# One ring of five for the raw and the lower halves of the weights, and the layer loop written out

## The reference

```python
for l in range(2):                                    # "the layers"
    a = hybrid_mixer(rms_norm(x), ...)                # MLA heads + dilated-window heads, w_in, w_uq, w_ukv, w_mix_out
    x = x + rms_norm(a)
    c = memory_cross_attention(rms_norm(x), mem, w_xq, w_xk, w_xv, w_xo)
    x = x + rms_norm(c)
    x = x + rms_norm(square(relu(rms_norm(x) @ w_up)) @ w_down)
...
# then one "second block": spatial gating + sparse attention with compressed keys,
# a memory attention and an MLP (w_ff1, w_ff2)
```

## Time and profile before

| | us |
|---|---|
| runs before | median 1491.85 of 3 (1487.62 to 1497.28) |
| span of the profiled execution | 1491.5 |
| device time of that same execution | not given apart; the median of the runs is 0.35 above the span |
| PE busy, DVE busy, ACT busy | 1339.5, 826.5, 665.9 |
| the layers and the second block, by their weights | to about 995, and from there |

### The profile page before, as it was taken

One profiled execution on the slowest core, in us unless ns is written; L12 is line 12 of the kernel. 1 busy time (PEld: TensorE's weight loads), 2 busy tenths in 40 slices (PEclk: granted clock), 3 DMA queues, 4 the chain that ended last, 5 costly groups with the idle time before them and its releaser, 6 DMA issues.

```text
span 1491.5 us, 24522 instructions
## 1 busy us (share of the span) xinstructions
PE 1339.5 (90%) x10217; PEld 1297.6 (87%) x10217; DVE 826.5 (55%) x872; ACT 665.9 (45%) x937; POOL 85.3 (6%) x65
## 2 busy tenths in 40 slices
PE   3998898889999899889888999989969888699999
PEld 3988897779999798889777999979969777699998
DVE  5476436456654547543645565456536765656542
ACT  5364334355543436433435454343234544355432
POOL 3000001020000100000202000003000000000000
PEclk7998999999999999889899999999659889899999
DMA  6633333235655533243333465565313123256553
GB/s 186 223 96 107 131 124 114 85 113 164 194 184 195 160 115 116 87 132 123 96 102 113 135 204 190 189 188 156 92 57 113 57 85 113 70 157 198 183 187 111
DMA packets 195585, 203.04 MB, mean 136 GB/s; under 512 B 5716, under 2 KB 191847, under 8 KB 195471
## 3 DMA queue, kind: packets, MB, share of 16 engines
q1 hardware_dynamic: 192704, 194.82, 40.8%
q0 software_dynamic: 2464, 5.99, 1.4%
q10 hardware_dynamic: 303, 0.61, 0.1%
HBM read 200.33 MB, written 3.16 MB: 136 GB/s over the span
## 4 chain that ended last, share of the span: by engine, by line
PE 75%; DVE 9%; ACT 8%; issue 6%; DMA 2%; POOL 0%; DVEq 0%; ACTq 0%; SPq 0%
PE bank L554 13%; PE bank L555 13%; PE bank L556 13%; PE bank L2033 6%; PE bank L2035 6%; PE bank L2031 6%; ACT w_hi L508 3%; PE bank L595 3%; DVE w_lo L518 3%; PE bank L596 2%; PE bank L597 2%; PE bank L1893 1%; PE bank L1954 1%; PE bank L1918 1%; DVE rstd L1251 1%
## 5 line engine op out<-in xcount | busy, mean ns | idle before, releaser
L518 DVE TENSOR_TENSOR w_lo<-raw,w_hi 128x2048 fp32r<-128x2048 f32 (+7 forms) x210 | 424.1, 2029 | 462.1 <-ACT w_hi L508 462.0
L508 ACT ACTIVATE w_hi<-raw 128x2048 fp32r<-128x2048 f32 (+7 forms) x210 | 354.7, 1703 | 481.1 <-PE bank L556 200.8
L554 PE MATMUL bank<-act_hi,w_hi 128*128 128x256 f32 x1096 | 313.2, 286 | 1.1 <-DVE act_lo L1718 1.1
L555 PE MATMUL bank<-act_lo,w_hi 128*128 128x256 f32 x1096 | 310.8, 284 | 0.0
L556 PE MATMUL bank<-act_hi,w_lo 128*128 128x256 f32 x1096 | 310.7, 283 | 0.0
L554 PEld LDWEIGHTS bank<-act_hi,w_hi 128*128 128x128 f32 x1096 | 211.0, 193 | 2.1 <-DVE act_lo L1718 1.9
L2031 PE MATMUL bank<-h_hi,w_hi 128*128 128x256 f32 x768 | 212.2, 276 | 0.0
L2033 PE MATMUL bank<-h_lo,w_hi 128*128 128x256 f32 x768 | 212.0, 276 | 0.0
L2035 PE MATMUL bank<-h_hi,w_lo 128*128 128x256 f32 x768 | 212.0, 276 | 0.0
L555 PEld LDWEIGHTS bank<-act_lo,w_hi 128*128 128x128 f32 x1096 | 211.1, 193 | 0.2
L556 PEld LDWEIGHTS bank<-act_hi,w_lo 128*128 128x128 f32 x1096 | 211.0, 193 | 0.0
(11 more groups left out here) (329 smaller groups left out, 2279.6 us busy)
## 6 DMA issues: line engine op xcount, KB each, us to landing
raw<-in_w_up_dram SPq DMA_DIRECT2D x32, 1024.0 KB, 5.4
raw<-in_w_down_dram SPq DMA_DIRECT2D x32, 1024.0 KB, 5.1
raw<-in_w_ff_dram SPq DMA_DIRECT2D x32, 1024.0 KB, 5.3
raw<-in_w_in_dram SPq DMA_DIRECT2D x23, 1024.0 KB, 5.3
raw<-in_w_xk_dram SPq DMA_DIRECT2D x8, 1024.0 KB, 5.1
raw<-in_w_xv_dram SPq DMA_DIRECT2D x8, 1024.0 KB, 5.1
raw<-in_w_mix_out_dram SPq DMA_DIRECT2D x8, 1024.0 KB, 5.2
raw<-in_w_xq_dram SPq DMA_DIRECT2D x8, 1024.0 KB, 5.1
```

The costliest lines, as they stand in the source:

```text
L508: ins = act.activation(d, r, ACT.Copy)
L518: ins = dve.tensor_tensor(d, r, h.bitcast(F32), ALU.subtract)
L554: pe.matmul(o, stat_hi, mov_hi, start=first, stop=False)
L555: pe.matmul(o, stat_hi, mov_lo, start=False, stop=False)
```

## The change

`raw` and `w_lo` become two names of the same memory, a ring of five slabs; `w_hi` stays a ring of three. DVE writes the lower half over the raw slab that it reads. Where the split rearranges columns (the seven kinds above) it can't be written in place: such a slab takes two places, one for raw and the next one for its lower half. A function counts this out beforehand for all 187 slabs. A place comes free when PE has used what lay in it, so SP's queue now waits on `slab_used` in place of `slab_lo`. With five places and no rearranged slab about, the load of slab s waits for used s-5; behind a rearranged one it waits for less distant ones. The table of the distances that result, from the function:

| slabs | the load waits for |
|---|---|
| layer, 0 to 2, and 16 to 63 | used s-5 |
| layer, 3 to 7, 14, 15 | used s-4 |
| layer, 8 and 9 | used 3 and 5 |
| layer, 10 | used 7 |
| layer, 11 and 12 | used 9, both |
| layer, 13 and 14 | used 10, both |
| second block, 4, 5, 6 | used 1, 2, 3 |
| second block, 7 | used 3 |

In layer 0 the first four loads wait for nothing. The loops over the layers are Python loops now, and all engines have straight code with constants in their waits. The order of the steps is the same on every engine.

```diff
-RAW = 2
-RING = 3
+HI_RING = 3
+LO_RING = 5
...
+def weight_places():
+
+    places, at, count, user = [], 0, [0] * LO_RING, [0] * LO_RING
+    for g in range(DEPTH * 64 + 59):
+        layer, s = min(g // 64, DEPTH), g - 64 * min(g // 64, DEPTH)
+        moved = s in ((3, 4, 9) if layer == DEPTH else (3, 9, 10, 11))
+        r, lo = at % LO_RING, (at + moved) % LO_RING
+        at += 1 + moved
+        count[r] += 2 if layer == DEPTH and s in (3, 4) else 1
+        places.append((r, lo, count[r], max(user[r], user[lo])))
+        user[r] = user[lo] = g + 1
+    return places
...
-        raw = sb("raw", [P, RAW, SLAB])
-        w_hi = sb("w_hi", [P, RING, SLAB], F32R)
-        w_lo = sb("w_lo", [P, RING, SLAB], F32R)
+        loads = ExitStack()
+        with loads:
+            raw = sb("raw", [P, LO_RING, SLAB], on=loads)
+        w_lo = sb("w_lo", [P, LO_RING, SLAB], F32R)
+        w_hi = sb("w_hi", [P, HI_RING, SLAB], F32R)
...
-            loads = s // RAW + 1 + (second(layer) and s >= 3)
-            act.wait_ge(raw_loaded[s % RAW], layer * (16 * 32) + 16 * loads)
-            if s >= 3:
-                last = s - 2 if second(layer) else {16: 16, 17: 14, 18: 15}.get(s, s - 2)
-                act.wait_ge(sig["slab_used"], value("slab_used", layer, last))
+            r, _, loads, _ = PLACES[64 * layer + s]
+            act.wait_ge(raw_loaded[r], 16 * loads)
+            if 64 * layer + s >= HI_RING:
+                act.wait_ge(sig["slab_used"], value("slab_used", layer, s - HI_RING + 1))
...
-                sp.wait_ge(sig["slab_lo"], value("slab_lo", layer, s - RAW + 1))
+                r, _, _, users = PLACES[64 * layer + s]
+                if users:
+                    sp.wait_ge(sig["slab_used"], users)
...
-            with sp.Fori(0, DEPTH) as layer:
+            for layer in range(DEPTH):
...
-            with act.Fori(0, DEPTH) as layer:
+            for layer in range(DEPTH):
```

More of the change, by code:

```diff
@@ L367, in build @@
         sig = {name: sem(name) for name in PER}
-        raw_loaded = [sem(f"raw_loaded{r}") for r in range(RAW)]
+        raw_loaded = [sem(f"raw_loaded{r}") for r in range(LO_RING)]
         i_load = {n: sem("i_" + n) for n in ("cst", "x", "mem", "gains", "pos", "relb", "rows", "skew", "toep", "gains_2",
@@ L488, in split_views, with of_hi, of_lo, of_raw @@
             return [(d[:, :, x0:x1], r[:, :, y0:y1]) for (x0, x1), (y0, y1) in pieces]
[L490 to L495, removed]
-        def split_hi(act, layer, s):
-            loads = s // RAW + 1 + (second(layer) and s >= 3)
-            act.wait_ge(raw_loaded[s % RAW], layer * (16 * 32) + 16 * loads)
-            if s >= 3:
-                last = s - 2 if second(layer) else {16: 16, 17: 14, 18: 15}.get(s, s - 2)
-                act.wait_ge(sig["slab_used"], value("slab_used", layer, last))
+        PLACES = weight_places()
+        def of_hi(layer, s):
+            return w_hi[:, (64 * layer + s) % HI_RING]
+        def of_lo(layer, s):
+            return w_lo[:, PLACES[64 * layer + s][1]]
+        def of_raw(layer, s):
+            return raw[:, PLACES[64 * layer + s][0]]
+        def split_hi(act, layer, s):
+            r, _, loads, _ = PLACES[64 * layer + s]
+            act.wait_ge(raw_loaded[r], 16 * loads)
+            if 64 * layer + s >= HI_RING:
+                act.wait_ge(sig["slab_used"], value("slab_used", layer, s - HI_RING + 1))
             pieces = split_views_2 if second(layer) else split_views
-            views = pieces(s if s < 64 else 0, w_hi[:, slot(layer, s)], raw[:, s % RAW])
+            views = pieces(s if s < 64 else 0, of_hi(layer, s), of_raw(layer, s))
             for n, (d, r) in enumerate(views):
@@ L515, in split_lo @@
             pieces = split_views_2 if second(layer) else split_views
-            for (d, r), (h, _) in zip(pieces(sp, w_lo[:, slot(layer, s)], raw[:, s % RAW]),
-                                      pieces(sp, w_hi[:, slot(layer, s)], raw[:, s % RAW])):
+            for (d, r), (h, _) in zip(pieces(sp, of_lo(layer, s), of_raw(layer, s)),
+                                      pieces(sp, of_hi(layer, s), of_raw(layer, s))):
                 ins = dve.tensor_tensor(d, r, h.bitcast(F32), ALU.subtract)
@@ L558, in w_view @@
         def w_view(layer, s, cols):
-            return (w_hi[:, slot(layer, s)].rearrange("p (k n) -> p k n", n=cols),
-                    w_lo[:, slot(layer, s)].rearrange("p (k n) -> p k n", n=cols))
+            return (of_hi(layer, s).rearrange("p (k n) -> p k n", n=cols),
+                    of_lo(layer, s).rearrange("p (k n) -> p k n", n=cols))
         def columns_slab(pe, layer, s, o, src_hi, src_lo, ready=None, first=True, last=True):
@@ L1367, in _ @@
             dve.wait_ge(i_evac, 8)
-            with dve.Fori(0, DEPTH) as layer:
+            for layer in range(DEPTH):
                 dve.tensor_copy(g_cur[:, :], g_all[:, layer, :]).then_inc(sig["gains"], 1)
@@ L1984, in slab @@
                     pe.wait_ge(sig["c_lo"], value("c_lo", layer, 5))
-                    wh = w_hi[:, slot(layer, s)].rearrange("p (a k n) -> p a k n", a=2, k=2)
-                    wl = w_lo[:, slot(layer, s)].rearrange("p (a k n) -> p a k n", a=2, k=2)
+                    wh = of_hi(layer, s).rearrange("p (a k n) -> p a k n", a=2, k=2)
+                    wl = of_lo(layer, s).rearrange("p (a k n) -> p a k n", a=2, k=2)
                     for m in range(4):
@@ L2039, in wh3 @@
             def wh3(layer, s):
-                return w_hi[:, slot(layer, s), 0:1536].rearrange("p (k n) -> p k n", k=3)
+                return of_hi(layer, s)[:, 0:1536].rearrange("p (k n) -> p k n", k=3)
             def wl3(layer, s):
-                return w_lo[:, slot(layer, s), 0:1536].rearrange("p (k n) -> p k n", k=3)
+                return of_lo(layer, s)[:, 0:1536].rearrange("p (k n) -> p k n", k=3)
             def kpe(layer, _):
@@ L2054, in _ @@
             steps = {"slab": slab, "pair": pair, "stat": stat, "kpe": kpe, "scores": scores, "turn": turn, "pv": pv, "ot": turn_o}
-            with pe.Fori(0, DEPTH) as layer:
+            for layer in range(DEPTH):
                 for kind, n in TE_ORDER:
@@ L2229, in slab_2 @@
                     pe.wait_ge(once["ch_lo"], 2)
-                    wh = w_hi[:, slot(DEPTH, s), 0:512].rearrange("p (k n) -> p k n", n=P)
-                    wl = w_lo[:, slot(DEPTH, s), 0:512].rearrange("p (k n) -> p k n", n=P)
+                    wh = of_hi(DEPTH, s)[:, 0:512].rearrange("p (k n) -> p k n", n=P)
+                    wl = of_lo(DEPTH, s)[:, 0:512].rearrange("p (k n) -> p k n", n=P)
                     for kind in range(2):
```

18 lines of the change are left out of this document (9 added, 9 removed).

## The result

The changed kernel takes 1514.16 us (median of 4 runs, 1510.34 to 1516.72) against 1493.11 for the kernel before in the same comparison (4 runs, 1487.62 to 1497.28). The ratio is 1.0152, with a 95% interval of 1.0127 to 1.0177: slower by 1.5%, 21 us. The forecast was 1503.0: the sign was right, the loss in the layers was foreseen and most of that in the second block was not, and the size was half of what came. The forecast gave 0.31 of chance to a loss of over 1%, and 0.64 to a result within 1%.

What follows compares the result with a forecast made beforehand. PE was taken to bound the kernel, busy 1339.5 of 1491.5 us. Terms 4.0 + 5.1 + 2.1 + 1.1 - 1.0 - 0.2 = 11.1 on the 1491.85 median gave 1503.0 us; 8-in-10 range 1487 to 1516.

Steps and rivals of the forecast that it cites:

- Layers, hi of 11 and 13: Layers: later loads delay these splits on ACT, and PE's pv 3 behind p_t 3; +4.0 in layer 0, +5.1 in layer 1.
- the rival in which it all vanishes: No change: PE's later idle time absorbs the layers' 4.0 and 5.1 us and the clock loss; 1491.8 us, chance 0.20.
- the 10.0 of my terms: Layers: late hi of 13 +4.0 and +5.1, clock +2.1, earlier loads -1.0 and -0.2.
- The clock, "+2.1": PE at slab 11: longer idling ahead lowers its granted clock, 1.6 us in layer 0 and 0.5 in layer 1.
- The second block, "+1.1": Second block: slab 5's late load delays hi of 5, cin_hi, toep's masking and PE's turning of toep, by 1.1 us.
- slack of 3.8 us: Second block: the first 3.8 us of slab 5's 4.9 us delay are covered by PE's own work before turning toep.
- Gains at slabs 18 and 19, "-1.0": Layers: earlier loads let hi of 19 start at slab 16's end, 0.5 us earlier in each layer.
- The in-place write, 0: DVE's lower-half splits: same instruction and shapes with output elsewhere, so no cost.
- The loop, 0 with bounds of -1 and +1: Layer loops written out: DVE's 2.57 us at the second round goes, but PE does not wait for it; 0.
- The base: Whole kernel: the forecast adds its terms to the median, 1491.85 us, 0.35 from the profiled span of 1491.5.
- The slower rival: Layers: two loads released at once share the transfer, the first landing 2.9 us later; 1515.5 us, chance 0.18.
- The faster rival: Last chain: its 18.3 us of loads are real waits and go; 1474 to 1486 us, chance 0.12.

Runs made afterwards that it cites:

- gain_late: The change, with POOL's 0.5 MB load into k_t moved behind its two scalings of the memory; 1510.65 us, ratio 1.0138 to the kernel before.
- late_second: loops_alone, with second-block loads of slabs 4 and 5 also waiting for used 1 and used 2; 1500.58 us, ratio 1.0087 to the kernel before.
- pt3_first: The change, with p_t 3 moved before hi of slab 13 on ACT in both layers; 1498.29 us, ratio 1.0029 to the kernel before.
- second_order: The change, with the second block's hi and lo of slab 5 moved further back on ACT and DVE; 1506.15 us, ratio 1.0088 to the kernel before.
- any_place: The change, but each load takes whichever place comes free first, a split rearranged slab's raw place included; 1490.14 us, ratio 0.9999 to the kernel before.
- loops_alone: The kernel before, old rings kept, with only its layer loops written out on every engine; 1494.05 us, ratio 1.0037 to the kernel before.
- late_layers: loops_alone, with both layers' loads of slabs 11 and 13 also waiting for used 9 and used 10; 1504.48 us, ratio 1.0108 to the kernel before.

## Why the prediction was half right

**Layers, hi of 11 and 13.** Right in mechanism and place, and in size for the waits. Forecast in layer 0: hi of 11 at 106.0, it was at 105.10; hi of 13 at 122.0, it was at 123.07, because slab 10 itself ran at a clock of 0.69 in place of 0.86 and ended 0.9 later, while the load took 5.3 us where I had given 5.15. In layer 1 hi of 13 slipped by 4.8 beyond what it inherited (forecast 5.1), the start of slab 10 by 1.1 (forecast 1.1). `pv` 3 waited 6.07 and 6.27 us, where I had said about 6. Behind it, 1.4 us of the delay were absorbed in each layer between the ends of slabs 11 and 12: the rival in which it all vanishes is refuted. That the layers as a whole lost 8.6 us, near the 10.0 of my terms, is in part luck. Layer 0 alone lost 9.5 where the terms give 5.1, and layer 1 ended 0.5 less behind than it began where they give 4.9: it was 3.3 us further behind at slab 13, and all of that was gone by slab 18.

**The clock, "+2.1".** This term was mis-sized: PE's busy time grew by 7.5. I had counted slab 11 alone, and forecast nothing for the second block, which lost 2.0 in slab 5 and 3.1 in slab 7. Slab 11 of layer 0 lost 2.5 (forecast 1.6). Part of this comes and goes without any cause in the change: slab 17 took 8.11 us before and 6.00 after in layer 1, and 6.00 before and 7.42 after in layer 0. Slab 7 may be such a case as well. It took 11.04 us in the change and in gain_late, and 7.9 in late_second, pt3_first and second_order; no wait stood just ahead of it, as PE ran from 1054.17 to its end with no gap of more than 0.1 us. What sets it is open, and a single profile can't tell how much is the change's.

**The second block, "+1.1".** This is the step that failed. By the profile 6.3 us were lost by the end of slab 5 and 12.2 over the whole block (7.2 behind at its start, 19.3 at its end), so the term fell 11.1 us short, more than the whole forecast did (19.3 against 11.1). Two things were missed. The load took 7.9 and not 5.15, since POOL's load for `k_t` was issued just before it; before the change that load lay between those of slabs 5 and 6. So the slack of 3.8 us that I found between hi of 5 and PE's turning of `toep` was used up by 2.7 more: forecast 4.9 late, measured 14.8 - 7.2 = 7.6. And I had followed only `cin_hi` behind hi of 5, not the squares of the first head, the step right behind it in the same queue, which PE needs as soon as slab 4 ends.

**Gains at slabs 18 and 19, "-1.0".** Hi of 18 no longer waits for a load and hi of 19 starts at used 16, as forecast: ACT's row ends its idle time with a matmul.

```profile
177.97 1.90 ACT L527 ACTIVATE w_hi<-raw 128x2048 fp32r<-128x2048 f32 x1
186.69 1.91 ACT L527 ACTIVATE w_hi<-raw 128x2048 fp32r<-128x2048 f32 x1 [6.82 <-PE bank L575]
```

PE's wait for the `p_t` behind hi of 19 fell from 1.73 to 1.59 us in layer 0 and from 1.87 to 1.31 in layer 1, 0.7 together where I had 1.0. By any_place against loops_alone all early loads together are worth 3.9 us (3 us of uncertainty on each), where I had 1.2; but loops_alone is the kernel whose loads of 18 and 19 were slow, and with early loads such a slow load has over 10 us to spare. One more wait went with the change and is in no term: before, hi of 16 waited for used 15 and not for used 13. It cost nothing in layer 0, where ACT came to hi of 16 at 166.49 and slab 15 was used at 162.22.

**The in-place write, 0.** Right: DVE's 210 splits took 424.0 us in all, 424.1 before.

**The loop, 0 with bounds of -1 and +1.** Open, see above; the upper bound was too tight for the one comparison that showed 5.05. The rule of the Trainium skill that I had weighed ("Runtime: NRT & Kernel Launch", "Instruction fetch mechanics": a taken branch can force a fetch) would have made straight code faster, and no run shows that. I had set the longer code's own loads aside because the trace shows no stall; the slow loads of slabs 18 and 19 in loops_alone say that they can matter, through a weight load and not as a stall.

**The base.** I took the median of the runs, 0.35 us above the span of the profiled execution. The runs show 1.8 between an execution's device time and its span (1512.68 for the profiled execution with its span of 1510.9). By that the profiled execution of before took an estimated 1493.3 us, and with 11.1 on top the forecast would have read 1504.4.

**The slower rival** named 1515.5, close to what came, but by luck: its mechanism is refuted. Loads 11 and 12 were issued 0.4 us apart; a view of the issues of that stretch:

```profile
raw<-in_w_ukv_dram SPq DMA_DIRECT2D x1, 1024.0 KB, 4.9
raw<-in_w_xk_dram SPq DMA_DIRECT2D x1, 1024.0 KB, 7.6
```

The first of a pair lands as if alone and the second takes 2.7 us longer: within SP's queue the older load is served first. The faster rival fell too: the old loads left the chain, and what they were worth was small. Its 18.3 us were a misreading besides: with slab 21 of layer 0 the loads of that chain add up to 24.5.

## What to carry to other kernels

When a wait is moved from one event to a later one, list every step that stands behind the waiting instruction in its queue, to the first one that the bounding engine needs, and not only the nearest. Look for other queues' transfers that the moved one will now meet. If the late load can't be helped, putting the needed step ahead of the split costs nothing and gave back all of the 1.5% here; a ring in which each load takes the place that comes free first gave it back too.

## What the runs showed of the hardware

A 1 MB load on SP's queue that was issued 0.8 us after a 0.5 MB load on POOL's took 7.9 us (7.5 in second_order, 7.6 in late_second), and 5.5 with that load out of its way. Two 1 MB loads of one queue, issued 0.4 us apart, landed after 4.9 and 7.6 us. With one packet of the queue called "instruction" in its first three microseconds, slab 18's load took 6.6 to 7.6 us in four cases, and 5.0 to 5.2 without one in eight. And the time that PE loses by waiting need not be the wait alone: slab 11 of layer 0, right behind the longer wait, ran at a granted clock of 0.68 in place of 1.00 and took 2.5 us more, in the change, in gain_late and in late_layers alike, with 8.2 us against 5.7.
